# Zero-padded 128-partition keys for the second block's score products, with the steps placed anew

## What is computed

```python
(mq, mk, mv, nq, nkc, nvc, nks, nvs, nkw, nvw, ngate,
 dq, dk, dv, sq, sk, sv) = split(rms_norm(x) @ w_in_2)
# moba: softmax(mq mk^T / 8 - alibi) mv, causal, 4 heads with own keys
# nsa:  gate0 * attention over 15 compressed keys
#     + gate1 * (nq nks^T) causal + gate2 * (nq nkw^T) causal, one key head for 4 query heads
# diff: each head has two 32-wide halves;
#       (softmax(q1 k1^T) - lam * softmax(q2 k2^T)) dv, then an RMS norm
# swa:  window of 128, 2 key heads for 4 query heads, with sinks
x = x + rms_norm(concat(o_moba, o_nsa, o_diff, o_swa) @ w_out_2)
x = x + rms_norm(conv_ffn(rms_norm(x)))
```

## Time and profile before

| | |
|---|---|
| median of 3 runs | 980.51 us (978.72, 980.51, 984.54) |
| the profiled execution | 978.22 us, span 976.4 us |
| PE busy | 953.5 us, 98% of the span |
| DVE, ACT, POOL busy | 612.7, 441.0, 309.5 us |
| granted TensorE clock, mean | 0.996 of 2.4 GHz |
| DMA share | 43.4% (queue of the weights) |

### The profile page before, as it was taken

One profiled execution on the slowest core, in us unless ns is written; L12 is line 12 of the kernel. 1 busy time (PEld: TensorE's weight loads), 2 busy tenths in 40 slices (PEclk: granted clock), 3 DMA queues, 4 the chain that ended last, 5 costly groups with the idle time before them and its releaser, 6 DMA issues.

```text
span 976.4 us, 16782 instructions
## 1 busy us (share of the span) xinstructions
PE 953.5 (98%) x6854; PEld 884.0 (91%) x6854; DVE 612.7 (63%) x1125; ACT 441.0 (45%) x827; POOL 309.5 (32%) x149
## 2 busy tenths in 40 slices
PE   9999999989999989999999999999899999999997
PEld 8879999979999879999999889988799999999996
DVE  6934866656765878534435667474877756776673
ACT  6443223554443485343344546565743533333333
POOL 3824111133010115232151193222344643404251
PEclk9999999999999999999999999999999999999999
DMA  8535232334233546555554335221545744455531
GB/s 307 183 130 209 97 126 95 123 108 140 106 108 130 194 171 246 209 190 176 180 205 177 126 135 174 97 81 66 195 153 192 259 173 174 175 214 179 186 110 43
DMA packets 23179, 154.80 MB, mean 159 GB/s; under 512 B 2608, under 2 KB 3120, under 8 KB 5440
## 3 DMA queue, kind: packets, MB, share of 16 engines
q1 hardware_dynamic: 22384, 151.58, 43.4%
q0 software_dynamic: 576, 2.10, 0.7%
q10 hardware_dynamic: 144, 0.07, 0.0%
HBM read 152.42 MB, written 1.05 MB: 157 GB/s over the span
## 4 chain that ended last, share of the span: by engine, by line
PE 88%; DVE 6%; ACT 4%; issue 1%; DMA 1%; SPq 0%; DVEq 0%; ACTq 0%
PE pb L501 86%; DVE wl L510 2%; PE pb L504 2%; DVE FA L510 2%; ACT wh L507 1%; ACT FA L507 1%; ACT R L507 1%; DMA sm<-in_sm 1%; DVE X L516 1%; DVE R L516 1%; DVE FA L516 0%; DVE wh L525 0%; SPq L537 0%; DVE FA L513 0%; ACT st L507 0%
## 5 line engine op out<-in xcount | busy, mean ns | idle before, releaser
L501 PE MATMUL pb<-R,wh 128*128 128x256 f32 (+1 forms) x3056 | 561.2, 285 | 8.5 <-ACT R L507 2.4
L501 PEld LDWEIGHTS pb<-R,wh 128*128 128x128 f32 x3056 | 476.9, 190 | 18.5 <-ACT FA L507 3.8
L510 POOL TENSOR_TENSOR wl<-raw,wh 128x1024 fp32r<-128x1024 f32 (+1 forms) x115 | 286.1, 2496 | 609.8 <-ACT wh L507 527.7
L501 PE MATMUL pb<-R,wl 128*128 128x256 f32 (+1 forms) x1528 | 428.3, 282 | 0.0
L510 DVE TENSOR_TENSOR wl<-raw,wh 128x1024 fp32r<-128x1024 f32 (+1 forms) x165 | 225.2, 1374 | 121.1 <-ACT wh L507 119.6
L501 PEld LDWEIGHTS pb<-R,wl 128*128 128x128 f32 x1528 | 289.7, 190 | 0.0
L507 ACT ACTIVATE wh<-raw 128x1024 fp32r<-128x1024 f32 (+1 forms) x229 | 236.2, 1047 | 110.6 <-PE pb L501 107.7
L501 PE MATMUL pb<-wh,R 128*128 128x512 f32 (+2 forms) x724 | 234.6, 389 | 4.1 <-DVE FA L510 1.6
L501 PEld LDWEIGHTS pb<-wh,R 128*128 128x128 f32 (+1 forms) x724 | 134.4, 186 | 36.0 <-DVE FA L510 2.0
L501 PE MATMUL pb<-wl,R 128*128 128x512 f32 (+2 forms) x372 | 144.2, 388 | 0.0
L507 ACT ACTIVATE FA<-pb 128x256 f32<-128x256 f32 (+7 forms) x155 | 66.9, 441 | 136.7 <-PE pb L501 115.1
(11 more groups left out here) (110 smaller groups left out, 475.0 us busy)
## 6 DMA issues: line engine op xcount, KB each, us to landing
raw<-in_w SPq DMA_DIRECT2D x138, 1024.0 KB, 4.8
X<-in_x SPq DMA_DIRECT2D x2, 512.0 KB, 4.3
raw<-in_w SPq DMA_DIRECT2D x2, 512.0 KB, 6.6
post<-in_ffn_post SPq DMA_DIRECT2D x2, 512.0 KB, 5.7
post<-in_w POOLq DMA_DIRECT2D x2, 512.0 KB, 3.9
FA<-in_w POOLq DMA_DIRECT2D x2, 512.0 KB, 4.3
out<-X SPq DMA_DIRECT2D x4, 256.0 KB, 2.0
cst<-in_cst SPq DMA_DIRECT2D x1, 797.0 KB, 12.7
```

Source lines behind the costliest of these rows:

```text
L501: return self.real.matmul(*a, **k) if self.real else self
L510: return self.real.tensor_tensor(*a, **k) if self.real else self
```

## The change

The 20 different key tiles of the 24 maps become tiles of 128 partitions that hold one head's keys (or one 32-wide half's) at their own place and zeros elsewhere. The queries are used as whole tiles, 128 partitions. 17 of the tiles lie where `R1` lies (free by then), three in `FA`. Who writes them:

- ACT: the evac of mk 0, mk 1 and s 2 and of the `slc`/`win` keys (`tm2_out`) is two instructions (Identity with a per-partition scale of zeros and ones) where it was one copy.
- POOL: after the evac of d 2 and d 3, four products each with such a column, and the df scores wait for all four.
- SP: the swaps across halves are now of two tiles each, 8 DMAs instead of 4; a score waits for its own tile's two.

The compressed branch (`cmp_score` with 64 partitions, `cmp_value` with 15, `cmp_hid` with 30 columns) is as before. `MADE` and all seven strings of `MIX` are other ones: by the letters p and q POOL splits 98 units where it split 113, but units 169 to 176, split within `maps`, are all p, where before 168, 170, 172, 173, 175 and 177 were p or q.

```diff
-               ("m1", T1), ("dmc", 256), ("dms", 256), ("cmpb", 120), ("rows", 2)]:
+               ("m1", T1), ("dmc", 256), ("dms", 256), ("cmpb", 120), ("rows", 6)]:
-    put("rows", np.stack([p < 64, p >= 64], 1))
+    put("rows", np.stack([p < 64, p >= 64] + [p // 32 == i for i in range(4)], 1))
-MADE = ("dpdpdpppppdpppvpdpdddpdpqqdvpdddpvddddppddpppvvdvddqpqdqvppdvvpdddvppddddpdddpddddvddvddpdpvddqp"
+MADE = ("dpdpddvddvdqppdddvdddpdvpddpdpvddqppqdddpvqvdpvdpppddpqvdddvpvdpvdvqdpdpqpdddpdppdddvdddddqdddqd"
...
     "maps":
-    ".....c.b.ecc...dfcbc.dagdffg.dfd.b.beacgbgcfaed.dfcghdehgeh.agiaege.afhb.abh..h.l.biac.f.aic.akm"
-    "lchiielhdedke.ibno.mn.bjbpoqjlejoqmnoljodninjpimkmqopmcepipk.qik.qqik..",
+    "........cae..ce.ab.gcdeggf.agbd.fadgf.e.fha.acbg.dabefdcbhhehcc.if.dfife..hcabehgabg.mdii.lei.ea"
+    "jbldc.cioh.hjedcdkmomknbb.komlqdnbpcinjlnjiqkmnopljkoeiqkp.qiq.opimp.q.",
...
+        names = [("moba", h) for h in range(4)] + [(m, i) for m in ("slc", "win") for i in range(2)] \
+            + [("swa", n, i) for n in range(2) for i in range(2)] + [("df", h, i) for h in range(4) for i in range(2)]
+        KEY = dict(zip(names, [keys[:, 256 * i:256 * i + 256] for i in range(17)] + more))
...
-            MAPS["moba", h] = dict(q=mq[r, n, :], k=mk[r, n, :], of=[("evac", "mq", n), ("evac", "mk", n)], bias=(0, h),
+            MAPS["moba", h] = dict(q=mq[:, n, :], k=KEY["moba", h], of=[("evac", "mq", n), ("evac", "mk", n)], bias=(0, h),
...
-                MAPS[m, h] = dict(q=dqk[r3, n, :], k=dqk[r3, 2 + n, :], of=[("evac", "d", n), ("evac", "d", 2 + n)],
+                MAPS[m, h] = dict(q=dqk[:, n, :], k=KEY["df", h, i], of=[("evac", "d", n)], apart=("apart", 2 + n),
...
+                    if M.get("apart"):
+                        e.wait_ge(*pool.at(M["apart"]))
+                    if M.get("moved"):
+                        e.wait_ge(*M["moved"].at("all"))
...
+                    elif name == "mk" or step == ("evac", "s", 2):
+                        e.wait_ge(*pe.at(use))
+                        for i in range(2):
+                            e.activation(KEY["moba", 2 * n + i] if name == "mk" else KEY["swa", i, i], b[:, 0:256], ACT.Identity,
+                                         scale=rows(i)).then_inc(*act.up(step))
...
-                    e.activation(nka, banks.of(("tm2", 2))[:, 0:256], ACT.Copy).then_inc(*act.up(("tm2_out", "k")))
+                    for i, m in enumerate(("slc", "win")):
+                        e.activation(KEY[m, i], banks.of(("tm2", 2))[:, 0:256], ACT.Identity,
+                                     scale=rows(i)).then_inc(*act.up(("tm2_out", "k")))
...
+                elif kind == "evac" and a in (("d", 2), ("d", 3)):
+                    e.wait_ge(*act.at(step))
+                    e.wait_ge(*in_cst.at("all"))
+                    n = a[1]
+                    for i in range(4):
+                        e.tensor_scalar(KEY["df", 2 * (n - 2) + i // 2, i % 2], dqk[:, n, :], rows(2 + i), None,
+                                        ALU.mult).then_inc(*pool.up(("apart", n)))
...
-                    e.dma_start(nkb[64:128, :], nka[0:64, :]).then_inc(*in_nkb[0].up("all", by=16))
-                    e.dma_start(nkb[0:64, :], nka[64:128, :]).then_inc(*in_nkb[1].up("all", by=16))
+                    for i, m in enumerate(("slc", "win")):
+                        moved(KEY[m, 1 - i], KEY[m, i], in_nkb[m])
```

More of the change, by code:

```diff
@@ L570, in program @@
         WL = [sb(f"wl{i}", 1024, FR) for i in range(NBASE)]
+        with nc.sbuf_tensor("keys", [128, 2 * 8 * T1], FP) as keys:
+            pass
         R1 = sb("R1", 2 * 8 * T1, FR)
@@ L594, in program @@
         in_w1 = [signal(f"in_w1_{i}") for i in range(2)]
-        in_nkb, in_s3, out_done = [signal(f"in_nkb{i}") for i in range(2)], [signal(f"in_s3{i}") for i in range(2)], signal("out_done")
-        every = [pe, act, dve, pool, in_xm, in_id, in_sm, in_cst, in_lev, out_done] + in_x + in_first + in_slab + in_w1 + in_nkb + in_s3 \
+        in_nkb, in_s3 = {m: signal("in_nkb_" + m) for m in ("slc", "win")}, [signal(f"in_s3{i}") for i in range(2)]
+        out_done = signal("out_done")
+        every = [pe, act, dve, pool, in_xm, in_id, in_sm, in_cst, in_lev, out_done] + in_x + in_first + in_slab + in_w1 + list(in_nkb.values()) + in_s3 \
             + list(in_post.values())
@@ L711, in program @@
         mq = fa(o, 512).rearrange("p (n t) -> p n t", n=2); o += 512
-        mk = fa(o, 512).rearrange("p (n t) -> p n t", n=2); o += 512
+        more = [fa(o + 256 * i, 256) for i in range(3)]; o += 768
         TM1 = fa(o, 1024).rearrange("p (c n) -> p c n", c=2); o += 1024
@@ L745, in program @@
             b0, n = 64 * (h % 2), h // 2
-            r = slice(b0, b0 + 64)
-            MAPS["moba", h] = dict(q=mq[r, n, :], k=mk[r, n, :], of=[("evac", "mq", n), ("evac", "mk", n)], bias=(0, h),
+            MAPS["moba", h] = dict(q=mq[:, n, :], k=KEY["moba", h], of=[("evac", "mq", n), ("evac", "mk", n)], bias=(0, h),
                                    scale=0.125, v=[TM1[:, c, 64 * h:64 * h + 64] for c in range(2)], vs="tm1_out")
             for m, gi, voff, same in (("slc", 1, 0, b0 == 0), ("win", 2, 64, b0 != 0)):
-                MAPS[m, h] = dict(q=nq[r, n, :], k=(nka if same else nkb)[r, :], of=[("evac", "nq", n)], swap=not same,
+                MAPS[m, h] = dict(q=nq[:, n, :], k=KEY[m, h % 2], of=[("evac", "nq", n), ("tm2_out", "k")],
+                                  moved=None if same else in_nkb[m],
                                   bias=(1, h), scale=0.125, v=[TM2[:, c, voff:voff + 64] for c in range(2)], vs="tm2_out",
@@ L1304, in scalar @@
                         banks.ended(use, act.now())
+                    elif name == "mk" or step == ("evac", "s", 2):
[3 more added lines that the diff above has]
+                                         scale=rows(i)).then_inc(*act.up(step))
+                        banks.ended(use, act.now())
                 elif kind == "hi_out":
@@ L2142, in slab, with moved @@
                 e.dma_start(raw[s % NRAW][:, :], dr["w"][s]).then_inc(*in_slab[s % NRAW].up(s, by=16))
+            def moved(dst, src, sig):
+                e.dma_start(dst[64:128, :], src[0:64, :]).then_inc(*sig.up("all", by=16))
+                e.dma_start(dst[0:64, :], src[64:128, :]).then_inc(*sig.up("all", by=16))
             def gains(name):
```

48 lines of the change are left out of this document (19 added, 29 removed).

## The result

The changed kernel takes **968.84 us** (median of 4 runs, 968.4 to 969.34), the kernel before 979.81 beside it (4 runs, 978.72 to 984.54): ratio 0.9879, 95% interval [0.9846, 0.9912]. The profiled executions are 978.22 us before and 968.40 after.

The account below looks back on a forecast made before the run. TensorE was taken to bound the kernel, busy 953.5 of 976.4 us; the score edges save 6.0 us, added work and reordering 0, so 980.5 - 6.0 = 974.5 us. The 8-in-10 range was 969.5 to 980.5.

Parts of the forecast that it names:

- The edges (6.0 us): 24 score steps of maps: late starts around 64- or 32-partition products go with full rows, saving 6.0 us.
- my bounds of 4.0 and 9.4: Score steps' saving: 9.4 us if every step stood alone, 4.0 if lost overlap and cmp_* neighbours take more back.
- Rival 4: Score steps: edges belong to fp32 products, not rows, so only overlap of two pairs is lost; 981.3 us, chance 0.04.
- POOL's keys: POOL's df key products after d 2 and d 3, 0.93 us each, in time with 1.3 us slack; cost 0.
- my upper end of 3.7: First df score in maps: if POOL's four key products are late, the price is between 0 and 3.7 us.
- ACT and SP at 0: Four more ACT evacuations (0.381 us each) and four more SP DMAs (landing in 2.0 us) cost 0.
- I take 0, between -3.1 and +3.1: Rewoven order: it can lose or gain a stall like that in maps, worth 3.1 us; no sign preferred.
- the event at 654 us: In maps: DVE's 2.20 us product beside POOL's split, PE stood 1.43 us, then 1.7 us clock loss; worth 3.1 us.
- The base of the forecast: Whole kernel: 6.0 us taken off the runs' median 980.5, which is 2.3 us above the profiled 978.22.
- Rival 1: In maps: larger gain, as the stall at 654 us goes too, worth 3.1 us; 971.4 us, chance 0.21.
- Rival 2: End of maps: some 5 of the 6 us saved return as waits of PE; 979.5 us, chance 0.19.
- Rival 3: In maps: POOL's products and splits block DVE's small products; two meetings cancel the gain, four give 986.9 us; chance 0.09.

Follow-up runs that it names:

- e7: The changed kernel in the old order, with ACT instead of POOL writing the df keys: 973.81 us, ratio 0.9941 to the kernel before.
- e1: The changed kernel with the old order (MADE and MIX strings of the kernel before): 979.91 us, ratio 0.9994 to the kernel before.
- e3: The changed kernel with both operands of every score product cut to 64 or 32 partitions, same order and keys: 986.78 us, ratio 1.0043 to the kernel before.
- e8: The changed kernel with only the last eight scores (swa and moba) cut back to 64 partitions: 973.88 us, ratio 0.9945 to the kernel before.
- e12: The changed kernel with the last eight scores on 64 partitions, second-block cmp_hid on 128 columns and cmp_value on 128 partitions: 970.07 us.
- e2: The kernel before with the new order (new MADE and MIX strings), old keys and sliced scores: 979.53 us, ratio 0.9981 to the kernel before.
- e16: The changed kernel with PE held at the score of moba 3 by a clearing on POOL: 969.72 us, ratio 0.9889 to the kernel before.
- e9: The changed kernel with PE held at the score of moba 3 for a small DMA: 978.63 us, ratio 1.0000 to the kernel before.

## Why the prediction was wrong

- **The edges (6.0 us): the right mechanism, about 0.9 us too large.** 5.1 measured (5.2 in the old order), inside my bounds of 4.0 and 9.4. The step alone has the length and the start that were worked out from the earlier trace rows, and its price, 0.36, is what I had read (0.34 to 0.39); eleven of them leave 1.2 us for the other thirteen, where I had 1.75. Rival 4 (edges of fp32 as such) is out, by the row at 589.07. That e7's 973.8 is so near the forecast of 974.5 is partly luck: between the profiles it gains 4.4 us, and the median of the kernel before stands 2 us above its profiled run.
- **POOL's keys: right, by less than I said.** Worked out: four products from 584.8 to 588.5, PE there at 589.8. Measured: 583.98 to 588.65, PE at 589.07, so 0.4 us of slack instead of 1.3. They took 1.17 us each, not 0.93, and biases plus DMAs ended at 577.8 (578.6). e1 shows the price when the cover is gone: 4.2 us of wait, over my upper end of 3.7, and 3.4 more in clock, which I had not counted.
- **ACT and SP at 0: right in the new order** (PE waits for neither before 668 us). ACT's scaled copies take 0.47 us, not the 0.381 of the earlier trace rows.
- **"I take 0, between -3.1 and +3.1": the step that failed.** Of the 9.9 us between the spans 5.1 are edges, so what I had put at 0 came to 4.8. The traces name 2.8 of it, in `maps`: 1.5 of waits (1.6 to 0.1) and 1.3 of half clock. I had named the event at 654 us, priced it about rightly (1.4 of wait, 1.7 of clock), and then said that no row prefers a sign. Two things were not in the sum. First, the event went with full rows in both orders (e1, e7, the changed kernel). DVE records drawn out beside POOL are even more frequent after (seven small ones longer than 0.6 us in `maps`, three before), but none reaches PE. Second, the rows themselves act on the clock: after the change no half clock stands in `maps`, and e3, e8 and e12 show that this hangs on the full rows. I had put the clock down to the stall alone. The other 2.0 us (1.3 in `maps`, 0.7 outside it) are not explained.
- **The base of the forecast.** The medians differ by 11.0 us, the profiles by 9.8. The runs of the kernel before, taken on four chips beside the experiments, are the longer the lower their mean clock: 978.1 to 979.6 us at 0.998, 978.8 to 981.1 at 0.994, 984.8 to 985.2 at 0.989. The changed kernel's four runs all have 0.996. So its median gains by the clock what the profiled pair doesn't show, and I had subtracted a saving without clock from a median with it.
- **Rival 1 (971.4) was nearest**, though its mechanism, one stall less, covers only 3.1 of the 5.7 us missing. That the new order could not do it alone is shown by e2. Rival 2 (given back at the end of `maps`) fell: the second half has no wait up to 668 us. Rival 3 (POOL against DVE) happens in e2, not in the changed kernel. The rule of the Trainium skill that the prediction names ("TensorE: Matmul & The Clock Gate", section "Why this matters for your kernels"), to put products with few rows on distinct row groups so that they run at once, loses here: e3, which brings that overlap back, is never under 976.7.

How far the account goes: shown are the edges (e3 against the changed kernel, e1 and e7 against the one before), POOL's wait (e1 against e7), and that slices bring half clock where full rows have none (e3, e8 against the changed kernel; e12). Open is which of the order's many moves is worth the 5 us between e7 and the changed kernel; nor is it settled why e12's 64-partition scores alone leave the clock up, whether by their number or by their distance (four runs, and it changes `cmp_value` and `cmp_hid` at once). The Trainium skill, "TensorE: Matmul & The Clock Gate", section "What's actually happening", says that the clock is set by how busy the PE has been lately. The falls that begin within the waits of e1 and e9 agree; the one of e3 at 652 us, with PE busy 12.00 of the 12.00 us ahead of it, shows that the profile's busy share is not that measure.

## What to carry to other kernels

Where small fp32 products on 64 or 32 partitions stand alone between full-array work, pad an operand with zeros and use all rows: 0.36 us for a step alone, 0.2 on average over the 24 here, more with its clock. Read the granted clock beside PE's busy share before pricing such an edit: a row with PE at 100% and clock at 0.5 to 0.6 is a loss that no wait names, and in e3's profile it was worth more than twice the edges. An edit that adds work to a queue and the order laid out for it have to be tried together: each alone measured nothing, both 11 us; with the work in another queue the edit alone measured 6.4 (e7). Late starts added up are no price: the steps around them make some of it good, and only the same order with and without the edit shows the sum.

## What the runs showed of the hardware that I had not expected

- The granted clock falls to 1.2 GHz with PE busy throughout (e3: 12.4 us lost in `maps`, e8: 9.2), and such a kernel's runs scatter by 10 to 16 us, where those with full rows and no long wait lie within some 1 to 4.
- At full rows a hold of 1.06 us cost 0.9 and no clock (e16); holds of 4.2 and 5.9 us ended in stretches of 6.8 and 10.2 us at half clock (e1, e9).
- A step with a stationary operand of 30 columns costs 0.27 us by its edges, one on 15 partitions 0.33, one on 64 or 32 partitions 0.36, when it stands alone.
- POOL's eight products of 128x256 with a column took 0.91 to 1.79 us each.
- A DMA of 0.2 KB issued 0.4 us behind a slab of 1024 KB in the same queue took 4.6 us to land (e9), where 64 KB land in 2.0.
